# Input norm: the first third of the first product placed behind the third token tile, and the second token tile loaded ahead of the spread norm weights

## The chip, the cores and the metric

The kernel runs on one core of a Trainium2 chip. The metric is device time in microseconds (us). The core has a matrix engine (TensorE, PE in the profile; its weight loads are listed apart as PEld), a vector engine (VectorE, DVE), a scalar engine (ScalarE, ACT), a general engine (GpSimd, POOL) and a queue engine (SyncE, SP) that issues most DMAs. Each engine takes its own instructions in the written order and meets the others at semaphores.

## The reference

One step of a one-layer encoder. 1024 prompt tokens and 8 x 16 sample tokens, 1152 in all with 2048 features, are normed and multiplied by one wide input projection. From its columns come the inputs of a windowed attention and of a gated linear attention; both results are gated, joined, multiplied by an output projection and added to the input. Only the first two lines below are touched by this case.

```python
def rmsnorm(x, g):
    xf = x.astype(jnp.float32)
    y = xf * lax.rsqrt(jnp.mean(xf * xf, axis=-1, keepdims=True) + EPS)
    return (y * g.astype(jnp.float32)).astype(x.dtype)

    xn = rmsnorm(x, norm_g)          # (1024 + 128) x 2048
    h = xn @ w_in                    # 2048 x 5648
    ...
    return x + mix @ w_out           # 2048 x 2048
```

## The kernel before, in words

The 1152 tokens are nine tiles of 128 (`NT` = 9, numbered 0 to 8 here). The projection is computed transposed: an *item* j is a block of 128 output columns, and it is accumulated in three *groups* n of 384 tokens (`TN`), that is of three tiles each, over 16 slices k of the 2048 features. The product is taken in three passes per slice (lines 1835 to 1837: high part by low part, low by high, high by high), since both operands are held as a high part and a remainder (`x_hi`, `x_lo`, `w_hi`, `w_lo`). So item 0 has 3 x 16 x 3 matmuls.

Before any item can run, the *input norm* has to norm and turn the tiles. The work on tile t goes through four engines:

- **SP** loads the tile (`load_x`, line 344) into one of three buffers; from tile 3 on it first waits until the tile three before has been turned.
- **ACT** sums its squares (line 1666, "sum of squares t").
- **DVE** turns the sum into the variance (line 1969, "variance t"), **POOL** makes the reciprocal root (line 1621), and **DVE** scales the tile by it and by the norm weights `g_row` (line 1976, "scaling t"). The norm weights are one row of memory, spread by the DMA over 128 partitions, so that this transfer is as large as a tile (1024 KB).
- **PE** transposes the tile in 16 steps (line 1812, "turn t"), four to each of four PSUM banks.
- **ACT** copies each bank rounded to `x_hi` (line 1656), and **DVE** subtracts that from the bank to get `x_lo` (line 1963, `low_halves`). Only then may the bank be written by the next turn: `turn_x` waits for the `x_lo` of the tile before, bank by bank.

What fixes the order: each engine's list is written out by hand. ACT does the four copies of tile t and then sum of squares t + 2. DVE does scaling t, the first two `x_lo` of tile t - 1, variance t + 1, and the last two `x_lo` of tile t - 1. PE does turn t, and from tile 3 on puts a *third* of a group behind each turn: slices 0 to 5, 6 to 10 and 11 to 15 (18, 15 and 15 matmuls; here third A, B, C). Group 0 of item 0, which needs only the tiles 0, 1 and 2, stands behind the turns 3, 4 and 5; group 1 behind the turns 6, 7 and 8; group 2 follows as a whole. POOL splits the first item's weights into high part and remainder in between (lines 548 and 552), one of four chunks behind each reciprocal root from tile 1 to tile 4. All of this takes the first 58 us; after it, PE goes through items and then through the output projection.

Of the kernel before, what the change touches and what calls it, by code (L numbers as in the profile page):

```python
# [24 lines left out]
NT = TOK // P  # L25
# [3 lines left out]
NG = TOK // TN  # L29
# [53 lines left out]
def project(nc, sem, dram):  # L83
# [6 lines left out]
    with ExitStack() as ctx:  # L90
# [61 lines left out]
        s_xlo = sem("s_xlo")  # L152
# [186 lines left out]
        def _(sp):  # L339

            def load_x(t):
                if t >= 3:
                    sp.wait_ge(s_xt, 4 * (t - 2) + 4)
                sp.dma_start(x_buf[t % 3], x_p[t * P:t * P + P, :] if t < NTP else x_s).then_inc(s_x[t % 3], 16)

            load_x(0)
            sp.dma_start(g_row, norm_g[0:1, :].to_broadcast([P, D_MODEL])).then_inc(s_norm, 16)
            load_x(1)
            sp.dma_start(consts_sb[:, :], consts[:, 0:C_MASK0]).then_inc(s_ident, 16)
            load_x(2)  # L350
            for q in range(4):
# [145 lines left out]
            for q in range(4):  # L497
                load_w(q + 2, (q + 1) * P + (Q0 + P), P)
                store_item(q + 1, (q + 1) * P + Q0, P)
                ks = slice(4 * q, 4 * q + 4)  # L500
# [744 lines left out]
        class decode_pe:  # L1245
# [5 lines left out]
            def levels(self):  # L1251
                logits, values, diagonal, keys, level, _, _ = linear_stages(self.pe, T, dec=True)
                stages = {2: logits, 13: linear_stages(self.pe, T - 1)[-1], 17: diagonal, 21: keys, 38: values}
                for i, step in enumerate((28, 33)):
                    stages[step] = lambda i=i: level(i)
                return stages
# [188 lines left out]
        b_kp = work[:, 7136:7392].rearrange("p (c n) -> p c n", c=2)  # L1445
        b_mx, b_mn, b_neg, b_sk, b_es, b_sum, b_den = (small[:, 8 + 2 * i:10 + 2 * i] for i in range(7))
        kb, _, sb_, pb, nb = ub
        ob = sb_

# [353 lines left out]
        def _(pe):  # L1803
            pe.wait_ge(s_ident, 16)

            def turn_x(t):
                pe.wait_ge(s_xn, t + 1)
                for b in range(4):
                    pe.wait_ge(s_xlo, 4 * t + (b + 1))
                    for k in range(4):  # L1810
                        c = (4 * b + k) * P
                        mm = pe.transpose(xt_bank[b][:, k * P:k * P + P], x_buf[t % 3][:, c:c + P], ident)
                    mm.then_inc(s_xt, 1)
# [7 lines left out]
            def group(j, n, norm=False, norm_before=False, stages={}, ks=range(KT), sum_at=6):  # L1821

                pe.wait_ge(s_staged, NG * j + (n + 1))
                for k in ks:
                    if n * KT + k in stages:
                        stages[n * KT + k]()
                    if n == 0 and k % 4 == 0:
                        pe.wait_ge(s_wready, 4 * j + (k // 4 + 1))
                    if n > 0 and k == 6 and norm:
                        sum_squares(j, n - 1)  # L1830
                    if n == 0 and k == sum_at and norm_before:
                        sum_squares(j - 1, NG - 1)
                    tok = slice(n * TN, n * TN + TN)
                    out = acc[n][:, 0:TN]
                    pe.matmul(out, w_lo[:, k, :], x_hi[:, k, tok], start=(k == 0), stop=False)  # L1835
                    pe.matmul(out, w_hi[:, k, :], x_lo[:, k, tok], start=False, stop=False)  # L1836
                    mm = pe.matmul(out, w_hi[:, k, :], x_hi[:, k, tok], start=False, stop=(k == KT - 1))  # L1837
                    if n == NG - 1 and k % 4 == 3:
                        mm.then_inc(s_wfree, 1)
                if n < NG - 1 and ks[-1] == KT - 1:  # L1840
                    mm.then_inc(s_acc, 1)

            def sum_squares(j, n):
                pe.wait_ge(s_sqlo, j * NG + (n + 1))
                pe.wait_ge(s_v, j * NG + (n + 1))
                pe.matmul(ss_bank[:, 0:TN], ones_r, sq_lo, start=True, stop=False)
                pe.matmul(ss_bank[:, 0:TN], ones_r, sq_hi, start=False, stop=True).then_inc(s_ssq, 1)
# [25 lines left out]


            THIRDS = [range(0, 6), range(6, 11), range(11, KT)]
            for t in range(NT):
                turn_x(t)
                if t >= NG:
                    pe.wait_ge(s_xlo, 4 * t + 4)
                    group(0, t // NG - 1, ks=THIRDS[t % NG])  # L1880
            pe.wait_ge(s_xlo, 4 * NT + 4)
            pe.wait_ge(s_ones, 1)
            group(0, NG - 1, stages={(NG - 1) * KT + 2: lambda: sum_squares(0, 0),
# [72 lines left out]
        def _(dve):  # L1956
            dve.sem_inc(s_v, 1)
            dve.sem_inc(s_xlo, 4)
            def low_halves(t, banks=range(4)):
                for b in banks:  # L1960
                    dve.wait_ge(s_xhi, 4 * t + (b + 1))
                    dst = x_lo[:, 4 * b:4 * b + 4, t * P:t * P + P]
                    dve.tensor_tensor(dst, xt_bank[b][:, :].rearrange("p (k n) -> p k n", k=4),
                                      x_hi[:, 4 * b:4 * b + 4, t * P:t * P + P].bitcast(F32),
                                      ALU.subtract).then_inc(s_xlo, 1)

            def variance(t):
                dve.wait_ge(s_ss, t + 1)
                dve.tensor_scalar(var[:, :], ss[:, t % 2:t % 2 + 1], 1.0 / D_MODEL, EPS, ALU.mult, ALU.add)\
                   .then_inc(s_var, 1)  # L1970

            variance(0)
            dve.wait_ge(s_norm, 16)
            for t in range(NT):
                dve.wait_ge(s_rstd, t + 1)
                dve.scalar_tensor_tensor(out=x_buf[t % 3], in0=x_buf[t % 3], scalar=rstd[:, 0:1],
                                         in1=g_row, op0=ALU.mult, op1=ALU.mult).then_inc(s_xn, 1)
                if t >= 1:
                    low_halves(t - 1, range(2))
                if t + 1 < NT:  # L1980
                    variance(t + 1)
                if t >= 1:
                    low_halves(t - 1, range(2, 4))
            low_halves(NT - 1)
            dve.wait_ge(s_ident, 16)
# [259 lines left out]
```

## Time and profile before

| | |
|---|---|
| median of 3 runs | 1792.86 us (1791.85 to 1793.93) |
| the profiled execution's own time | 1792.29 us |
| its span, first to last instruction | 1790.5 us |
| PE busy | 1765.8 us (99%) |
| DVE, POOL, ACT busy | 781.5, 529.1, 505.2 us |
| mean granted TensorE clock | 0.996 |

PE is busy nearly all the time; the page's slices show a single one that stands out, the first (45 us), with PE at 6 tenths and its granted clock at 8 tenths. Engine times are busy times, and work on different engines overlaps. In a timeline, each row gives a start and a length, merged rows the length of the whole stretch, and the bracket tells how long the engine had been idle and which instruction let it go on. A row of PE ends later than the next one starts, since matmuls are pipelined.

### The profile page before, as it was taken

What the parts mean: (1) busy time and instruction counts of PE and PEld (TensorE: products, weight loads), DVE (VectorE), ACT (ScalarE), POOL (GpSimd) and SP (SyncE); (2) the same over time, 40 slices, a digit from 0 to 9 for tenths busy, and PEclk for the clock granted to TensorE, in tenths of its full rate; (3) what the DMA queues carried; (4) which work ended last, traced back from release to release, by engine and by line L of the source; (5) the groups of instructions that cost most, each with busy time, mean ns of one, the idle gap of its engine ahead of it and who ended that gap; (6) DMA issues with size and microseconds to landing.
All of it is one profiled execution on the core that took longest, in us unless ns stands there. A gap on an engine that the chain in (4) does not pass through costs nothing.

```text
span 1790.5 us, 29954 instructions
## 1 busy us (share of the span) xinstructions
PE 1765.8 (99%) x10741; PEld 1639.3 (92%) x10741; DVE 781.5 (44%) x1641; ACT 505.2 (28%) x1155; POOL 529.1 (30%) x486
## 2 busy tenths in 40 slices
PE   6999999999999999999999999999999999999999
PEld 5999999989999999999999999999999888888887
DVE  7754540554545421111556566552322453453433
ACT  6311110134333310000344434330011443343332
POOL 4356420322232242332655555552433000000000
PEclk8999999999999999999999999999999999999999
DMA  7432211343444332212333432334534675664654
GB/s 257 141 92 66 86 48 52 91 113 95 111 109 126 93 96 71 77 55 75 98 99 90 121 101 85 99 120 150 155 118 139 200 243 164 211 222 165 199 165 136
DMA packets 246128, 220.81 MB, mean 123 GB/s; under 512 B 26018, under 2 KB 210676, under 8 KB 244596
## 3 DMA queue, kind: packets, MB, share of 16 engines
q1 hardware_dynamic: 171828, 176.68, 31.4%
q10 hardware_dynamic: 74232, 43.23, 8.8%
q8 instruction: 42, 0.69, 0.2%
q14 instruction: 26, 0.21, 0.0%
HBM read 169.71 MB, written 52.24 MB: 124 GB/s over the span
## 4 chain that ended last, share of the span: by engine, by line
PE 96%; DVE 1%; DMA 1%; ACT 1%; ACTq 0%; issue 0%; POOL 0%; SPq 0%; DVEq 0%; POOLq 0%
PE p L1835 20%; PE p L1837 19%; PE p L1836 19%; PE p L1926 7%; PE p L1928 7%; PE p L1930 7%; PE p L901 2%; PE p L592 1%; PE p L1870 1%; PE p L1869 1%; PE p L1871 1%; PE p L620 1%; PE p L604 1%; PE p L913 1%; PE p L919 1%; PE p L912 1%
## 5 line engine op out<-in xcount | busy, mean ns | idle before, releaser
L1835 PE MATMUL p<-x_hi,w_lo 128*128 128x384 f32 x2016 | 697.6, 346 | 0.0
L1837 PE MATMUL p<-x_hi,w_hi 128*128 128x384 f32 x2016 | 675.3, 335 | 0.0
L1836 PE MATMUL p<-x_lo,w_hi 128*128 128x384 f32 x2016 | 674.3, 334 | 0.0
L1835 PEld LDWEIGHTS p<-x_hi,w_lo 128*128 128x128 f32 x2016 | 378.8, 188 | 15.6 <-issue 13.5
L548 POOL TENSOR_TENSOR w_hi<-raw,small 128x512 fp32r<-128x512 f32 x164 | 173.5, 1058 | 726.8 <-PE p L1837 710.8
L1836 PEld LDWEIGHTS p<-x_lo,w_hi 128*128 128x128 f32 x2016 | 379.1, 188 | 0.2
L1837 PEld LDWEIGHTS p<-x_hi,w_hi 128*128 128x128 f32 x2016 | 378.3, 188 | 0.0
L2137 DVE TENSOR_TENSOR w_lo<-raw,w_hi 128x512 fp32r<-128x512 f32 x192 | 132.1, 691 | 206.9 <-ACT w_hi L1783 206.9
L552 POOL TENSOR_TENSOR w_lo<-raw,w_hi 128x512 fp32r<-128x512 f32 x164 | 216.2, 1318 | 12.8
L1783 ACT ACTIVATE w_hi<-raw 128x512 fp32r<-128x512 f32 x192 | 120.8, 631 | 242.6 <-PE p L1930 213.1
L1926 PE MATMUL p<-w_hi,x_lo 128*128 128x512 f32 x570 | 160.2, 389 | 0.0
L1928 PE MATMUL p<-w_lo,x_hi 128*128 128x512 f32 x570 | 160.1, 389 | 0.0
L1930 PE MATMUL p<-w_hi,x_hi 128*128 128x512 f32 x570 | 160.1, 389 | 0.0
L1926 PEld LDWEIGHTS p<-w_hi,x_lo 128*128 128x128 f32 x570 | 106.9, 188 | 22.5 <-DVE w_lo L2137 0.4
L1928 PEld LDWEIGHTS p<-w_lo,x_hi 128*128 128x128 f32 x570 | 107.0, 188 | 22.3
L1930 PEld LDWEIGHTS p<-w_hi,x_hi 128*128 128x128 f32 x570 | 107.0, 188 | 22.2
L2023 DVE RECIPROCAL xn<-xn 128x384 f32<-128x384 f32 x30 | 76.6, 2553 | 18.9 <-ACT xn L1684 18.9
L2040 DVE TENSOR_TENSOR xn<-xn 128x384 f32<-128x384 f32 (+1 forms) x48 | 41.5, 879 | 99.1 <-ACT xn L1689 99.1
L2006 DVE COPY xn<-p 128x384 f32<-128x384 f32 x36 | 20.1, 557 | 132.6 <-PE p L1837 117.5
L1689 ACT ACTIVATE xn<-p 128x384 f32<-128x384 f32 x48 | 22.6, 491 | 175.5 <-PE p L1837 175.4
L745 DVE CUSTOM_DVE_ANT_0 work<-p,work,sink_row 128x192 f32<-128x192 f32 x128 | 45.7, 413 | 30.1 <-PE p L592 28.0
L679 ACT ACTIVATE work<-p 128x384 f32<-128x384 f32 x64 | 31.5, 492 | 91.5 <-PE p L605 91.3
(191 smaller groups left out, 1784.1 us busy)
## 6 DMA issues: line engine op xcount, KB each, us to landing
raw<-in_w_out SPq DMA_DIRECT2D x192, 256.0 KB, 3.5
raw<-in_w_in SPq DMA_DIRECT2D x164, 256.0 KB, 4.3
h_t<-xn SPq DMA_DIRECT2D x126, 192.0 KB, 1.9
work<-h_t SPq DMA_DIRECT2D x24, 384.0 KB, 6.1
out<-work SPq DMA_DIRECT2D x36, 256.0 KB, 4.6
work<-h_t ACTq DMA_DIRECT2D x16, 512.0 KB, 4.6
work<-h_t ACTq DMA_DIRECT2D x32, 256.0 KB, 4.2
work<-in_x_prompt SPq DMA_DIRECT2D x32, 256.0 KB, 4.9
```

What stands on the lines that cost most here:

```text
L548: pool.tensor_tensor(w_hi[:, k:k + 4, 0:n], w_raw(j, k, n), zeros[:, :].unsqueeze(1) .to_broadcast([P, 4, n]), ALU.add).then_inc(s_whi, 1)
L552: pool.tensor_tensor(w_lo[:, k:k + 4, 0:n], w_raw(j, k, n), w_hi[:, k:k + 4, 0:n].bitcast(F32), ALU.subtract).then_inc(s_wready, 1)
L745: dve.tensor_tensor_reduce(out=a_p[i][:, r, :], in0=bank_s[r % 2][:, (r // 2) * SPAN:(r // 2) * SPAN + SPAN], in1=a_mask[:, 2 * (r % 2), : ...
L1783: act.activation(o_hi[k % 4], o_raw[k % 4], ACT.Copy).then_inc(t_whi, 1)
L1835: pe.matmul(out, w_lo[:, k, :], x_hi[:, k, tok], start=(k == 0), stop=False)
L1836: pe.matmul(out, w_hi[:, k, :], x_lo[:, k, tok], start=False, stop=False)
L1837: mm = pe.matmul(out, w_hi[:, k, :], x_hi[:, k, tok], start=False, stop=(k == KT - 1))
L1926: pe.matmul(out[t], x_lo[:, k, tok[t]], o_hi[k % 4], start=(k == 0), stop=False)
L1928: pe.matmul(out[t], x_hi[:, k, tok[t]], o_lo[k % 4], start=False, stop=False)
L1930: mm = pe.matmul(out[t], x_hi[:, k, tok[t]], o_hi[k % 4], start=False, stop=(k == KT - 1))
L2023: dve.reciprocal(stage[n], tmp_b).then_inc(s_nchain, 1)
L2137: dve.tensor_tensor(o_lo[k % 4], o_raw[k % 4], o_hi[k % 4].bitcast(F32), ALU.subtract)\
```

## The change

Three lists are rewritten; no instruction is added or removed.

```diff
             load_x(0)
+            load_x(1)
             sp.dma_start(g_row, norm_g[0:1, :].to_broadcast([P, D_MODEL])).then_inc(s_norm, 16)
-            load_x(1)
...
             THIRDS = [range(0, 6), range(6, 11), range(11, KT)]
-            for t in range(NT):
+            for t in range(NG):
                 turn_x(t)
-                if t >= NG:
-                    pe.wait_ge(s_xlo, 4 * t + 4)
-                    group(0, t // NG - 1, ks=THIRDS[t % NG])
+            pe.wait_ge(s_xlo, 4 * NG + 4)
+            group(0, 0, ks=THIRDS[0])
+            turn_x(3)
+            group(0, 0, ks=THIRDS[1])
+            turn_x(4)
+            turn_x(5)
+            group(0, 0, ks=THIRDS[2])
+            for t in range(2 * NG, NT):
+                turn_x(t)
+                pe.wait_ge(s_xlo, 4 * t + 4)
+                group(0, 1, ks=THIRDS[t % NG])
...
             for t in range(NT):
+                if t == NG:
+                    low_halves(t - 1)
                 dve.wait_ge(s_rstd, t + 1)
                 dve.scalar_tensor_tensor(out=x_buf[t % 3], in0=x_buf[t % 3], scalar=rstd[:, 0:1],
                                          in1=g_row, op0=ALU.mult, op1=ALU.mult).then_inc(s_xn, 1)
-                if t >= 1:
+                if t >= 1 and t != NG:
                     low_halves(t - 1, range(2))
                 if t + 1 < NT:
                     variance(t + 1)
-                if t >= 1:
+                if t >= 1 and t != NG:
                     low_halves(t - 1, range(2, 4))
```

On the SP queue, at the start of the program, the second tile (buffer `raw`) and the spread norm weights change places:

```order
 L344 DMA work<-in_x_prompt 128x2048
-L347 DMA work<-in_norm_g 128x2048
 L344 DMA raw<-in_x_prompt 128x2048
+L348 DMA work<-in_norm_g 128x2048
 L349 DMA consts_sb<-in_consts 128x260
```

The second transfer is now the tile, the third the norm weights; both are of the same size.

On PE, from the end of turn 2 (buffer `xn`) on, where p_3 to p_6 are the banks of a turn and p_0 is the accumulator of group 0. Before:

```order
L1812 MATMUL p_5<-consts_sb,xn 128x128 x4
L1812 MATMUL p_6<-consts_sb,xn 128x128 x4
L1812 MATMUL p_3<-consts_sb,work 128x128 x4
L1812 MATMUL p_4<-consts_sb,work 128x128 x4
L1812 MATMUL p_5<-consts_sb,work 128x128 x4
L1812 MATMUL p_6<-consts_sb,work 128x128 x4
L1835 MATMUL p_0<-x_hi,w_lo 128x384
L1836 MATMUL p_0<-x_lo,w_hi 128x384
```

And the same place now:

```order
L1812 MATMUL p_5<-consts_sb,xn 128x128 x4
L1812 MATMUL p_6<-consts_sb,xn 128x128 x4
L1835 MATMUL p_0<-x_hi,w_lo 128x384
L1836 MATMUL p_0<-x_lo,w_hi 128x384
L1837 MATMUL p_0<-x_hi,w_hi 128x384
L1835 MATMUL p_0<-x_hi,w_lo 128x384
L1836 MATMUL p_0<-x_lo,w_hi 128x384
L1837 MATMUL p_0<-x_hi,w_hi 128x384
```

Third A, 18 matmuls, moved from behind turn 3 to ahead of it; third B moved from behind turn 4 to ahead of it in the same way.

On PE, two tiles later, at the turns 4 (buffer `raw`) and 5 (buffer `xn`). Before:

```order
L1836 MATMUL p_0<-x_lo,w_hi 128x384
L1837 MATMUL p_0<-x_hi,w_hi 128x384
L1812 MATMUL p_3<-consts_sb,xn 128x128 x4
L1812 MATMUL p_4<-consts_sb,xn 128x128 x4
L1812 MATMUL p_5<-consts_sb,xn 128x128 x4
L1812 MATMUL p_6<-consts_sb,xn 128x128 x4
L1835 MATMUL p_0<-x_hi,w_lo 128x384
```

And now:

```order
L1812 MATMUL p_3<-consts_sb,raw 128x128 x4
L1812 MATMUL p_4<-consts_sb,raw 128x128 x4
L1812 MATMUL p_5<-consts_sb,raw 128x128 x4
L1812 MATMUL p_6<-consts_sb,raw 128x128 x4
L1812 MATMUL p_3<-consts_sb,xn 128x128 x4
L1812 MATMUL p_4<-consts_sb,xn 128x128 x4
L1812 MATMUL p_5<-consts_sb,xn 128x128 x4
L1812 MATMUL p_6<-consts_sb,xn 128x128 x4
L1835 MATMUL p_0<-x_hi,w_lo 128x384
```

Before, third B stood between the turns 4 and 5; now the two turns stand next to each other. From turn 6 on the list is what it was.

On DVE, around scaling 3 (buffer `work`). Before:

```order
L1969 TENSOR_SCALAR small<-small 128x1
L1963 TENSOR_TENSOR x_lo<-p_5,x_hi 128x4x128
L1963 TENSOR_TENSOR x_lo<-p_6,x_hi 128x4x128
L1976 SCALAR_TENSOR_TENSOR work<-work,small 128x2048
L1963 TENSOR_TENSOR x_lo<-p_3,x_hi 128x4x128
L1963 TENSOR_TENSOR x_lo<-p_4,x_hi 128x4x128
L1969 TENSOR_SCALAR small<-small 128x1
L1963 TENSOR_TENSOR x_lo<-p_5,x_hi 128x4x128
L1963 TENSOR_TENSOR x_lo<-p_6,x_hi 128x4x128
L1976 SCALAR_TENSOR_TENSOR raw<-raw,small,work 128x2048
```

And now, where the lines have moved down by 8 and 10:

```order
L1977 TENSOR_SCALAR small<-small 128x1
L1971 TENSOR_TENSOR x_lo<-p_5,x_hi 128x4x128
L1971 TENSOR_TENSOR x_lo<-p_6,x_hi 128x4x128
L1971 TENSOR_TENSOR x_lo<-p_3,x_hi 128x4x128
L1971 TENSOR_TENSOR x_lo<-p_4,x_hi 128x4x128
L1971 TENSOR_TENSOR x_lo<-p_5,x_hi 128x4x128
L1971 TENSOR_TENSOR x_lo<-p_6,x_hi 128x4x128
L1986 SCALAR_TENSOR_TENSOR work<-work,small 128x2048
L1977 TENSOR_SCALAR small<-small 128x1
L1986 SCALAR_TENSOR_TENSOR raw<-raw,small,work 128x2048
```

All four `x_lo` of tile 2 stand ahead of scaling 3 now, and scaling 4 follows scaling 3 with only a variance between them.

## Rows read from the trace of the kernel before

**Rows 1.** The page of the kernel before: busy time and share by engine.

```profile
PE 1765.8 (99%) x10741; PEld 1639.3 (92%) x10741; DVE 781.5 (44%) x1641; ACT 505.2 (28%) x1155; POOL 529.1 (30%) x486
```

**Rows 2.** Waits of PE, 0 to 150 us: engine, line, releaser: total, times, longest.

```profile
PE p L1812 <- DVE work L1976: 11.2, 1, 11.2
PE p L1812 <- DVE x_lo L1963: 6.2, 4, 2.6
```

**Rows 3.** Timeline of PE: start, length, engine, line, operation, [idle before <- releaser].

```profile
11.21 3.44 PE L1812 MATMUL p<-consts_sb,work 128*128 128x128 f32 x16 [11.21 <-DVE work L1976]
...
22.58 3.65 PE L1812 MATMUL p<-consts_sb,xn 128*128 128x128 f32 x16 [2.60 <-DVE x_lo L1963]
...
27.63 3.91 PE L1812 MATMUL p<-consts_sb,work 128*128 128x128 f32 x16 [1.40 <-DVE x_lo L1963]
...
31.21 0.49 PE L1835 MATMUL p<-x_hi,w_lo 128*128 128x384 f32 x1
...
34.50 1.91 PE L1812 MATMUL p<-consts_sb,raw 128*128 128x128 f32 x16
...
38.86 2.32 PE L1812 MATMUL p<-consts_sb,xn 128*128 128x128 f32 x16
...
40.93 0.42 PE L1835 MATMUL p<-x_hi,w_lo 128*128 128x384 f32 x1
...
43.63 2.26 PE L1812 MATMUL p<-consts_sb,work 128*128 128x128 f32 x16
```

**Rows 4.** Timeline of PE, 55 to 60 us: first matmul of item 0's group 2.

```profile
57.70 0.33 PE L1835 MATMUL p<-x_hi,w_lo 128*128 128x384 f32 x1
```

**Rows 5.** Windows: length, busy (x) of five engines, granted clock, DMA.

```profile
16.00:18.00 2.00, 1.16 (x8) 0.83 (x8) 1.92 (x5) 1.84 (x4) 1.92 (x2) 0.93 0.77 137
18.00:20.00 2.00, 1.97 (x8) 1.57 (x8) 1.84 (x2) 1.07 (x2) 1.92 (x4) 0.50 1.00 418
...
30.00:32.00 2.00, 2.00 (x12) 2.00 (x11) 2.00 (x2) 1.23 (x3) 1.92 (x2) 0.66 0.14 57
```

**Rows 6.** Timeline of DVE, 0 to 80 us.

```profile
8.76 2.35 DVE L1976 SCALAR_TENSOR_TENSOR work<-work,small 128x2048 f32<-128x2048 f32 x1 [0.84 <-POOL small L1621]
...
18.72 3.12 DVE L1976 SCALAR_TENSOR_TENSOR xn<-xn,small,work 128x2048 f32<-128x2048 f32 x1 [0.16 <-POOL small L1621]
...
24.21 2.67 DVE L1976 SCALAR_TENSOR_TENSOR work<-work,small 128x2048 f32<-128x2048 f32 x1
...
28.79 0.15 DVE L1969 TENSOR_SCALAR small<-small 128x1 f32<-128x1 f32 x1 [0.70 <-ACT work L1666]
...
35.36 2.34 DVE L1976 SCALAR_TENSOR_TENSOR xn<-xn,small,work 128x2048 f32<-128x2048 f32 x1
...
39.19 1.28 DVE L1963 TENSOR_TENSOR x_lo<-p,x_hi 128x512 fp32r<-128x512 f32 x2
...
45.10 2.34 DVE L1976 SCALAR_TENSOR_TENSOR raw<-raw,small,work 128x2048 f32<-128x2048 f32 x1
...
52.07 4.91 DVE L1963 TENSOR_TENSOR x_lo<-p,x_hi 128x512 fp32r<-128x512 f32 x8
```

**Rows 7.** Timeline of ACT, 0 to 80 us.

```profile
10.71 1.91 ACT L1666 ACTIVATE work<-raw 128x2048 f32<-128x2048 f32 x1 [2.98 <-DMA raw<-in_x_prompt]
...
15.18 1.90 ACT L1666 ACTIVATE work<-xn 128x2048 f32<-128x2048 f32 x1
...
37.06 1.94 ACT L1666 ACTIVATE work<-work 128x2048 f32<-128x2048 f32 x1
```

**Rows 8.** Timeline of POOL, 0 to 80 us.

```profile
16.90 1.27 POOL L552 TENSOR_TENSOR w_lo<-work,w_hi 128x512 fp32r<-128x512 f32 x1
...
19.77 3.21 POOL L552 TENSOR_TENSOR w_lo<-work,w_hi 128x512 fp32r<-128x512 f32 x1
```

**Rows 9.** SP, when it issues a transfer: start, length, line.

```profile
1.21 0.42 SPq L347 DMA_DIRECT2D work<-in_norm_g  x1
```

**Rows 10.** DMA issues, 0 to 30 us: KB each, median us to landing.

```profile
work<-in_norm_g SPq DMA_DIRECT2D x1, 1024.0 KB, 7.0
```

## The prediction

> **What bounds the kernel now.** I read the page first: PE is busy 99% of the span [rows 1], so time can only be won or lost where PE stands idle or slow. The waits of PE over the first 150 us name only two causes: 11.2 us until scaling 0 on DVE is done, and 6.2 us in four waits for `x_lo`, also DVE [rows 2]. Both lie inside the input norm. The timeline of PE places them: idle to 11.21, 2.60 ahead of turn 2, 1.40 ahead of turn 3, then an unbroken stream, third A from 31.21, turn 4 at 34.50, turn 5 at 38.86, third C from 40.93, turn 6 at 43.63 [rows 3], and group 2 of item 0 at 57.70 [rows 4]. From that point PE does not wait in these rows, so the whole question is at what time group 2 of item 0 starts after the change. A shift of that start moves the end one for one.
>
> The second thing to see is the clock. It was granted at 0.50 (1.2 GHz) in 18 to 20 us, after two us in which PE had been busy for 1.16, and it rose inside 30 to 32 us (mean 0.66) [rows 5], at the end of turn 3, after 3.6 us without a pause. A turn of 16 transposes took 3.44 and 3.65 us early on and 1.91 us afterwards [rows 3]: 0.215 against 0.119 us each. I call 0.86 and 0.48 us the slow and fast time of a bank.
>
> The third thing is the loop that feeds PE. For each tile DVE needs a scaling (2.34 us alone, 2.67 and 3.12 elsewhere), four `x_lo` (eight in 4.91 us, 0.61 each) and a variance (0.15) [rows 6]. From scaling 5 at 35.36 to scaling 7 at 45.10 is 9.74 us, 4.87 a tile [rows 6]; PE spends 1.91 us of turn and about 2.8 us of third. The two are nearly level, so DVE has no slack to give back a delay.
>
> **The first edit, the norm weights behind tile 1.** SP issues the spread weights at 1.21 and they land 7.0 us later, at 8.2 [rows 9, 10]; tile 1, next in line and as large, lands at 10.71, where ACT ends its wait for it [rows 7]. Scaling 0 started at 8.76, with POOL's root as its last releaser [rows 6]. With the places swapped I let the landings swap: tile 1 at 8.2, weights at 10.7. Scaling 0 then runs from 10.7 to 13.1 instead of 8.76 to 11.1, and turn 0, which began at 11.21, from 13.15 to 16.6. The earlier tile 1 buys nothing: its sum of squares was not what PE waited for.
>
> Most of those 2 us survive. Sum of squares 2 stands on ACT behind the copies of turn 0: 15.18 becomes 17.3 (last bank 16.6, plus copy) and it ends at 19.3 [rows 7]. Variance 2 waits for it (as a variance did for ACT at 28.79, 0.70 us [rows 6]), and DVE's second pair of `x_lo` of tile 0 is queued behind that variance: 19.4 to 20.7. Scaling 2 goes from 18.72 to 20.7 [rows 6], turn 2 from 22.58 to 24.4, ending at 27.9 at the slow clock. Cost so far 1.8 us. Below, it could cost nothing if the three transfers landed together by 8.8; above, the whole 2.45 us between the two landings.
>
> **The second edit, third A ahead of turn 3.** It takes the place of the 1.40 us wait, and this is its gain. But it needs all `x_lo` of tile 2, so DVE does these four first: the last copy of turn 2 ends at 28.6 (27.9 plus 0.1 plus 0.6), the last `x_lo` at 29.2. Third A starts at 29.2 and scaling 3 too, 5.0 us later than its 24.21 [rows 6], ending by 31.8 under cover of third A. Third A's 18 matmuls took 3.29 us at the fast clock (31.21 to 34.50 [rows 3]). If the clock rises near 31.3 again, 2.1 us of it run slow; no row shows such a matmul slow, so I scale by the transposes, 0.18 times 1.8 gives 0.33 each: six are done by 31.3, the other twelve take 2.1. Third A ends at 33.3 and turn 3 at 35.2. Before, the same two pieces were done at 34.50: 0.7 us late. The bounds of this term are 0.4 us (all fast: 29.2 + 3.3 = 32.5, then turn 3 to 34.4, a gain of 0.1 against before) and all slow, 29.2 + 5.9, 1.8 us more than I take.
>
> **The third edit, turns 4 and 5 side by side.** This is the largest term. Third B goes ahead of turn 4, 35.2 to 37.9 (2.7 us, as 36.2 to 38.9 before). Scaling 4 is no obstacle: 32.7 to 35.3. Behind the copies of turn 3 (to 35.9) ACT does sum of squares 5 to 37.9; variance 5 and the second pair of `x_lo` of tile 3 follow at 38.1 to 39.3, so turn 4 ends at 39.8 and scaling 5 runs from 39.3 to 41.65 instead of from 35.36 [rows 6]. Before, turn 4 and third B were done at 38.86: 0.9 us late.
>
> Turn 5 now needs three things in a row that nothing covers: scaling 5, then the first `x_lo` of tile 4 (42.25), then, behind sum of squares 6 (40.4 to 42.4) and variance 6, the second pair, to 44.2, and a last bank of 0.48. It ends at 44.7. Before, the same loop ran from the end of turn 4 (34.50 + 1.91 = 36.4) to third C at 40.93, 4.5 us, with 2.7 us of third B inside it; sum of squares 6 at 37.06 and the pair at 39.19 are its links [rows 6, 7]. Now it is 4.9 us from 39.8 with nothing inside: PE is idle 2.4 us and then waits between banks. Third C (40.93 to 43.63, 2.7 us) ends at 47.4 instead of 43.63: 3.7 us late.
>
> **The rest.** The list from turn 6 on is unchanged, and DVE sets the pace. Scaling 6 stands behind the pair that ends at 44.2; scaling 7 comes 4.7 later at 48.9; from scaling 7 to the last block of `x_lo` it was 45.10 to 52.07, 6.97 us, so 55.9; the four of tile 7 take 2.45, the last bank of turn 8 another 0.5, third C 2.7. Group 2 starts at 61.5 instead of 57.70. The weight load of item 1 waits for turn 7, and its split for group 2 itself, so they move along.
>
> Sum: 61.5 - 57.7 = **3.8 us**. Against the profiled execution that is 1792.29 + 3.8 = 1796.1. The median of before is 0.57 above that execution, and the measured median is what the new one will be held against, so I predict 1792.86 + 3.8 = **1796.7 us**, 0.21% slower. About 0.2%, 3.6 us, is what can be told from no change here, so the forecast sits on that edge.
>
> **A rule weighed.** Scaling 2 took 3.12 us and POOL's subtraction beside it 3.21, while the same forms took 2.35 and 1.27 at other places [rows 6, 8]. The Trainium skill, GPSIMD Engine Reference, section Specifications, says that POOL shares its memory interfaces with VectorE and contends with instructions that read two SBUF operands, as a scaling does and an `x_lo`, with one operand in PSUM, does not. The trace agrees (3.12 against 2.35). By that rule scaling 2 stays slow at its new place, since POOL's next split starts behind root 2 at about 20, and the sum stays 3.8; without it the chain to turn 2 would be 0.8 shorter and the sum near 3.0.
>
> **Rivals.**
>
> *The clock falls again.* It fell once after the gap ahead of turn 1 [rows 5]. Around turn 5 PE would now be idle for 2.4 us and half idle for another 2.4. Third C at the slow clock costs 2.2 us more (2.7 times 0.8), parts of turns 5 and 6 another 0.5 to 1.5. Group 2 then starts 2 to 4 us later still: 1799 to 1800. Against it: between the turns of 38.86 and 43.63 small waits did no harm. Chance 0.20.
>
> *The clock rises early.* Turn 2 from 24.4 to 27.9 has no pause and third A follows within 1.3 us; if it rises there, third A and turn 3 are 1 us shorter, and part of it reaches turn 4 and 5. Or the weights land sooner than 10.7. Sum 1.5 to 2.9, 1794.4 to 1795.8. Chance 0.25.
>
> *The chain is hidden anyway.* If PE had enough work stored up that the DVE chain has slack, nothing changes: 1792 to 1794. The level pace (4.87 against 4.7) speaks against it. Chance 0.08.
>
> *Faster.* PE-bound mechanism: the third fills the wait of 1.40 ahead of turn 3, and by keeping PE busy from turn 2 on raises the clock before turn 3, which then takes 1.91 instead of 3.65: 1.4 + 1.7 = 3.1 us, 1789.7. It decides from the point where the weights land by 8.8 and the loop between turns 4 and 5 closes within 2.4 us instead of 4.5. Neither is in the rows. Chance 0.06.
>
> *The forecast*, 3.0 to 5.0 us, 0.41.
>
> **How the numbers follow.** Slower by over 0.2% (above 1796.4): 0.20 from the falling clock, and 0.31 of the forecast's 0.41, in all 0.51. Faster: 0.05. The rest, 0.44, within 0.2%. The range takes in the forecast, most of the falling clock and most of the early rise: 1793.8 to 1799.8.
>
> **What the new profile would show.** Right: scaling 0 near 10.7 with the weights as its releaser; turn 0 near 13.1; scaling 3 near 29 and third A at the same time; a PE gap of over 2 us ahead of turn 5, waiting for scaling 5 or `x_lo`; group 2 near 61.5. Wrong: scaling 0 at 8.8 (the landings do not swap), turn 5 close behind turn 4, or a granted clock below 1.00 between 40 and 48 us (the first rival).

## The result

The changed kernel took 1795.57 us (median of 20 runs, 1794.39 to 1798.29) against 1793.33 us for the kernel before (20 runs, 1791.46 to 1794.43). The ratio is 1.0015, 95% interval 1.0009 to 1.0021: 2.7 us slower by the ratio (1.6 to 3.8), 2.24 us by the medians. 1796.7 us and +3.8 us had been forecast. The direction is clear of noise, the size about two thirds of the forecast. It lies below the forecast's own 3.0 to 5.0 us and inside the 1.5 to 2.9 us of the rival in which the clock rises early. Of the 20 runs, the twelve with a mean granted clock of 0.997 took 1794.39 to 1796.17 us, and the eight with 0.995 or 0.996 took 1796.28 to 1798.29; the execution profiled below is one of the twelve.

The profiled execution took 1795.21 us with a span of 1793.4 us. Its timeline of PE, where the rows of before stand in [rows 3]:

```profile
13.17 3.65 PE L1812 MATMUL p<-consts_sb,work 128*128 128x128 f32 x16 [13.17 <-DVE work L1986]
...
24.06 3.65 PE L1812 MATMUL p<-consts_sb,xn 128*128 128x128 f32 x16 [2.31 <-DVE x_lo L1971]
...
29.12 0.44 PE L1835 MATMUL p<-x_hi,w_lo 128*128 128x384 f32 x1 [1.41 <-DVE x_lo L1971]
...
32.35 1.91 PE L1812 MATMUL p<-consts_sb,work 128*128 128x128 f32 x16
...
36.71 2.33 PE L1812 MATMUL p<-consts_sb,raw 128*128 128x128 f32 x16
41.32 3.53 PE L1812 MATMUL p<-consts_sb,xn 128*128 128x128 f32 x16 [2.29 <-DVE x_lo L1971]
```

Turn 0 starts at 13.17 (before 11.21), turn 2 at 24.06 (22.58), third A at 29.12 ahead of turn 3, turn 3 at 32.35 (27.63), turn 4 at 36.71 (34.50), turn 5 at 41.32 after an idle time of 2.29 us (38.86, with none). The first matmul of group 2, 57.70 in [rows 4], is now at 61.28:

```profile
61.28 0.33 PE L1835 MATMUL p<-x_hi,w_lo 128*128 128x384 f32 x1
```

The timeline of DVE, answering to [rows 6]:

```profile
10.72 2.35 DVE L1986 SCALAR_TENSOR_TENSOR work<-work,small 128x2048 f32<-128x2048 f32 x1 [2.94 <-DMA work<-in_norm_g]
...
19.38 0.15 DVE L1977 TENSOR_SCALAR small<-small 128x1 f32<-128x1 f32 x1 [2.02 <-ACT work L1666]
...
20.64 2.67 DVE L1986 SCALAR_TENSOR_TENSOR xn<-xn,small,work 128x2048 f32<-128x2048 f32 x1
...
28.98 2.34 DVE L1986 SCALAR_TENSOR_TENSOR work<-work,small 128x2048 f32<-128x2048 f32 x1
...
32.05 3.12 DVE L1986 SCALAR_TENSOR_TENSOR raw<-raw,small,work 128x2048 f32<-128x2048 f32 x1 [0.66 <-POOL small L1621]
...
36.97 0.15 DVE L1977 TENSOR_SCALAR small<-small 128x1 f32<-128x1 f32 x1 [0.60 <-ACT work L1666]
...
38.24 2.34 DVE L1986 SCALAR_TENSOR_TENSOR xn<-xn,small,work 128x2048 f32<-128x2048 f32 x1
...
47.41 0.15 DVE L1977 TENSOR_SCALAR small<-small 128x1 f32<-128x1 f32 x1 [0.92 <-ACT work L1666]
```

Scaling 0 has a new releaser, the norm weights, and starts at 10.72 instead of 8.76. Two waits are new to DVE, or in a new place: 0.66 us for POOL's root 4 ahead of scaling 4 (32.05), and 0.60 us for ACT's sum of squares 5 (36.97). Scaling 5 starts at 38.24 instead of 35.36. ACT no longer waits 2.98 us for tile 1 [rows 7], which has landed by 8.22:

```profile
8.22 1.91 ACT L1666 ACTIVATE work<-raw 128x2048 f32<-128x2048 f32 x1 [0.62 <-DMA raw<-in_x_prompt]
```

The clock took another course than before. It fell near 21.0 us, was back near 27.8, and fell a second time inside 40 to 42, right behind the gap ahead of turn 5; for before see [rows 5], a fall near 18 and a rise near 31.

```profile
20.00:22.00 2.00, 1.56 (x8) 0.98 (x8) 2.00 (x3) 1.13 (x3) 1.92 (x3) 0.75 0.49 205
...
26.00:28.00 2.00, 1.71 (x8) 1.30 (x7) 1.68 (x3) 1.45 (x3) 1.48 (x2) 0.55 0.00 0
...
40.00:42.00 2.00, 0.68 (x4) 0.71 (x5) 2.00 (x5) 1.55 (x2) 0.09 (x1) 0.87 0.95 299
42.00:44.00 2.00, 2.00 (x11) 2.00 (x10) 2.00 (x3) 1.19 (x2) 0.46 (x1) 0.50 0.54 225
```

So 3.58 us of delay stand at group 2, but the spans differ by 2.9 us only. Part of it is given back much later. In the timeline of the weight loads of PE, one attention unit (line 620) stands at 411.97 and the next at 427.12 in before, and between them PE waited 0.45 us for ACT:

```profile
411.97 0.85 PEld L620 LDWEIGHTS p<-work 128*64 128x64 f32 x16 [0.25 <-issue]
...
424.54 0.20 PEld L604 LDWEIGHTS p<-consts_sb,work 128*128 128x128 f32 x2 [0.45 <-ACT work L679]
...
427.12 0.85 PEld L620 LDWEIGHTS p<-work 128*64 128x64 f32 x16 [0.25 <-issue]
```

In the changed kernel the same two stand at 415.55 and 430.37, with no such wait between them; the shift goes from 3.58 to 3.25 us:

```profile
415.55 0.85 PEld L620 LDWEIGHTS p<-work 128*64 128x64 f32 x16 [0.25 <-issue]
...
430.37 0.85 PEld L620 LDWEIGHTS p<-work 128*64 128x64 f32 x16 [0.25 <-issue]
```

### The profile page after: what moved, and what is told of

Its sections match the earlier page's. It is cut to its first block, busy times and chain, and to the rows that moved or that the text cites. A ratio compares the mean times of both kernels' runs of the same rounds, so it can differ in the third digit from the quotient of the medians.

```text
span 1793.4 us, 29952 instructions
## 1 busy us (share of the span) xinstructions
PE 1765.2 (98%) x10741; PEld 1639.5 (91%) x10741; DVE 781.2 (44%) x1641; ACT 504.5 (28%) x1155; POOL 526.8 (29%) x486
## 4 chain that ended last, share of the span: by engine, by line
PE 96%; DVE 1%; ACT 1%; DMA 1%; issue 0%; ACTq 0%; POOL 0%; SPq 0%; DVEq 0%; POOLq 0%
PE p L1835 20%; PE p L1837 19%; PE p L1836 19%; PE p L1934 7%; PE p L1936 7%; PE p L1938 7%; PE p L901 2%; PE p L592 1%; PE p L1870 1%; PE p L1869 1%; PE p L1871 1%; PE p L1812 1%; PE p L620 1%; PE p L604 1%; PE p L919 1%; PE p L913 1%
## 5 line engine op out<-in xcount | busy, mean ns | idle before, releaser
L2050 DVE TENSOR_TENSOR xn<-xn 128x384 f32<-128x384 f32 (+1 forms) x48 | 41.5, 879 | 99.3 <-ACT xn L1689 99.3
L679 ACT ACTIVATE work<-p 128x384 f32<-128x384 f32 x64 | 31.4, 491 | 91.1 <-PE p L605 91.0
```

## The experiments

For each kernel I read two numbers: its median, beside a kernel before run on the same chip, and the start of the first sum-of-squares matmul of group 2 of item 0 (line 1846), here "the mark". It is at 58.74 in before and 62.32 in the changed kernel, and nothing of the input norm comes after it on PE:

```profile
58.74 0.33 PE L1846 MATMUL p<-sq_parts 128*128 128x384 f32 x1
```

```profile
62.32 0.33 PE L1846 MATMUL p<-sq_parts 128*128 128x384 f32 x1
```

**1. The load order alone.**

```diff
             load_x(0)
+            load_x(1)
             sp.dma_start(g_row, norm_g[0:1, :].to_broadcast([P, D_MODEL])).then_inc(s_norm, 16)
-            load_x(1)
```

> Only the first edit: tile 1 is loaded ahead of the spread norm weights, the lists of PE and DVE are those of before. My step (the swap delays scaling 0 by 2 us and 1.8 us of that reach turn 2, and the DVE loop behind it has no slack): scaling 0 starts near 10.7, turn 2 near 24.2, group 2 of item 0 at 58.9 to 59.5 instead of 57.7, time 1.2 to 1.8 us above before. Rival (the early delay is taken up by the waits of 2.60 and 1.40 us ahead of turns 2 and 3): turn 3 stays near 27.6 and the time is within 0.5 us of before.

Measured: 1794.96 us against 1792.90, ratio 1.0012 (1.0003 to 1.0021). Turn 2 at 23.79, and turn 3 did not stay near 27.6:

```profile
23.79 3.65 PE L1812 MATMUL p<-consts_sb,xn 128*128 128x128 f32 x16 [1.91 <-DVE x_lo L1963]
29.13 3.64 PE L1812 MATMUL p<-consts_sb,work 128*128 128x128 f32 x16 [1.69 <-DVE x_lo L1963]
```

The mark is at 60.24, 1.50 us late. The step of the prediction holds (1.8 us expected at turn 2, 1.2 seen there; 1.2 to 1.8 us expected in time, about 2.1 measured, 0.5 to 3.8 by the interval of the ratio). The rival falls.

**2. The edits of PE and DVE alone** (the changed kernel with the loads of before).

```diff
             load_x(0)
-            load_x(1)
             sp.dma_start(g_row, norm_g[0:1, :].to_broadcast([P, D_MODEL])).then_inc(s_norm, 16)
+            load_x(1)
```

> Only the edits of PE and DVE: third A behind turn 2, third B behind turn 3, turns 4 and 5 side by side, all x_lo of tile 2 ahead of scaling 3; the norm weights are loaded ahead of tile 1 as before. My step (these cost about 2 us by themselves): third A starts near 27.4, scaling 3 near 27.3, a gap of over 2 us ahead of turn 5, time 1.0 to 2.5 us above before. Rival (the swap is the whole loss, and filling the wait of 1.40 us ahead of turn 3 is a gain): within 0.3 us of before or faster by up to 1.4 us.

Measured: 1795.12 us against 1792.90, ratio 1.0009 (1.0000 to 1.0019).

```profile
27.70 0.69 PE L1835 MATMUL p<-x_hi,w_lo 128*128 128x384 f32 x1 [1.41 <-DVE x_lo L1971]
...
32.60 1.91 PE L1812 MATMUL p<-consts_sb,work 128*128 128x128 f32 x16
```

Third A started at 27.70, but at the slow clock, so that turn 3 could start only at 32.60, later than in the full change (32.35), whose third A started 1.4 us later on a fast clock. The mark is at 62.63. The medians differ by 2.2 us (1.0 to 2.5 expected), and by the interval of the ratio by 0 to 3.4. The edits cost something by themselves, as forecast; but two parts that cost about 2 us each and about 2.2 together do not add up. The course of the clock lies over both.

**3. Third B back between turns 4 and 5**, on the kernel of experiment 2.

```diff
             turn_x(3)
-            group(0, 0, ks=THIRDS[1])
             turn_x(4)
+            group(0, 0, ks=THIRDS[1])
             turn_x(5)
```

> As the kernel with only the edits of PE and DVE, but with third B back between turns 4 and 5. Theory of the prediction (the side by side turns uncover the loop of turn 4, its copies, sum of squares 6, x_lo, turn 5, and that is the largest term): the gap of over 2 us ahead of turn 5 goes, third B runs inside it, and the time is 1.5 to 2.7 us below that kernel, so no slower than before. Rival (scaling 3, pushed behind the four x_lo of tile 2, moves the whole chain of DVE back by 3 us and the chain is what bounds; where third B stands only moves the idle time): the gap appears ahead of turn 4 instead, and the time is within 0.7 us of that kernel.

Measured: 1794.28 us against 1792.90, ratio 1.0007 (0.9998 to 1.0016), 0.8 us below experiment 2 and within the noise of the ratios: between what the two theories said (1.5 to 2.7 us, and within 0.7). The mark is at 61.08, 1.55 us earlier, at the edge of the first. The gap ahead of turn 5 went, but gaps ahead of turn 4 and inside it came in its place, as the rival had it:

```profile
34.56 1.17 PE L1812 MATMUL p<-consts_sb,raw 128*128 128x128 f32 x8 [1.66 <-DVE x_lo L1971]
36.41 1.97 PE L1812 MATMUL p<-consts_sb,raw 128*128 128x128 f32 x8 [0.69 <-DVE x_lo L1971]
```

PE was fast during third A here (18 matmuls from 27.76 to 30.99) and slow at its start in experiment 2 (27.70 to 32.60), so this pair does not decide.

**4. PE kept busy in the gap ahead of turn 5**, on the changed kernel.

```diff
+            def keep_busy(n):
+                for _ in range(n):
+                    pe.transpose(ss_bank[:, 0:P], ident, ident)
...
             turn_x(4)
+            keep_busy(16)
             turn_x(5)
```

> The changed kernel with 16 further transposes of the identity matrix, into a bank that nobody reads at that time, between turns 4 and 5; they fill the gap of 2.3 us in which the changed kernel's PE stood idle before its granted clock fell to 0.50 at 41.7 us. Clock theory: the clock stays at 1.00 through turn 5 and third C, turn 5 takes about 2.3 us instead of 3.53, and the time falls by 0.8 to 1.4 us against the changed kernel, to 1.0 to 1.6 us above before. Rival (the chain of DVE paces the turns whatever the clock): the clock stays up and the time is within 0.4 us of the changed kernel, 2.0 to 2.8 us above before.

Measured: 1795.51 us against 1792.90, ratio 1.0019 (1.0010 to 1.0028). In the profiled execution the clock stayed up:

```profile
40.00:42.00 2.00, 1.46 (x14) 1.13 (x12) 2.00 (x5) 1.67 (x2) 0.00 (x0) 1.00 0.92 283
42.00:44.00 2.00, 2.00 (x15) 1.58 (x15) 2.00 (x3) 1.84 (x4) 0.55 (x1) 1.00 0.58 242
```

The mark came at 61.42, 0.90 us earlier than 62.32, of the size expected. In time nothing is seen, 1795.51 against 1795.57 for the changed kernel in another session, and 2.6 us above before, where the rival had 2.0 to 2.8: the stretch from the mark to the end of the span is 1.2 us longer in this execution than in the changed kernel's (1732.3 against 1731.1). Four of its eleven runs lie at 1797 to 1798.5, with a mean granted clock of 0.996 or 0.997, and seven at 1795.1 to 1795.8, with 0.998; where the four lost the clock was not profiled. The experiment shows the clock's price at this one place, not a gain.

**5 to 8. The clock taken out of the comparison.** The same device, with more transposes, ahead of every long gap of PE, on four orders of work, run one after the other on one chip. First the kernel before:

```diff
                 turn_x(t)
+                if t < NG:
+                    keep_busy((8, 12, 10)[t])
```

> The kernel before with 8, 12 and 10 further transposes of the identity matrix behind turns 0, 1 and 2, into a bank nobody reads then, so that PE has no long gap from turn 0 on. Clock theory: the granted clock, once up, stays at 1.00; turns 2 and 3 and third A run at the fast rate, and the first sum-of-squares matmul of group 2, at 58.74 in before, comes 0.5 to 1.6 us earlier; the time is 0.5 to 1.6 us below before. Rival (the added transposes delay the turns as much as the clock gives): within 0.4 us of before.

Then the edits of PE and DVE without that of the loads:

```diff
             for t in range(NG):
                 turn_x(t)
+                keep_busy((8, 12, 6)[t])
...
             turn_x(4)
+            keep_busy(16)
             turn_x(5)
```

> The kernel with only the edits of PE and DVE (norm weights ahead of tile 1), with 8, 12, 6 and 16 further identity transposes behind turns 0, 1, 2 and 4, so that the clock is out of the comparison with the kernel before with such transposes. Theory A (side by side turns, 2.7 us uncovered): the sum-of-squares matmul comes 2 us or more behind that one's. Theory B (scaling 3 pushed back behind the x_lo of tile 2, partly caught up by DVE since PE's third A fills the wait): 0.8 to 1.5 us behind it. Theory C (all of the loss of the PE and DVE edits was the clock): within 0.3 us.

Then the same with third B back between turns 4 and 5:

```diff
             turn_x(3)
-            group(0, 0, ks=THIRDS[1])
+            keep_busy(12)
             turn_x(4)
-            keep_busy(16)
+            group(0, 0, ks=THIRDS[1])
             turn_x(5)
```

> As the previous kernel but with third B back between turns 4 and 5, and 8, 12, 6 and 12 further identity transposes behind turns 0, 1, 2 and 3. Theory A (side by side turns are the loss): its sum-of-squares matmul comes 1.5 to 2.7 us earlier than in the previous kernel. Theory B (the chain of DVE bounds, whatever stands between turns 4 and 5): within 0.4 us of it, and the idle time of PE lies ahead of turn 4 instead of turn 5.

And the whole change, the second of these with the loads swapped:

> The changed kernel in full, with 8, 12, 6 and 16 further identity transposes behind turns 0, 1, 2 and 4; against the kernel that differs from it only in loading the norm weights ahead of tile 1, this prices the first edit without the clock. My step (1.8 us at turn 2 that all survive): its sum-of-squares matmul comes 1.4 to 2.0 us later than there. Rival (the price of the swap is mostly hidden): within 0.5 us.

| kernel, with added transposes | median us (11 runs each) | mark | clock of the profiled run |
|---|---|---|---|
| 5. before | 1790.78 (1790.35 to 1791.58) | 57.40 | 1.000 |
| 6. edits of PE and DVE | 1791.98 (1791.64 to 1793.56) | 59.00 | 1.000 |
| 7. the same, third B back | 1792.54 (1791.55 to 1793.69) | 58.95 | 1.000 |
| 8. the whole change | 1793.51 (1793.34 to 1794.09) | 60.55 | 1.000 |

Plain before in the same session: 1793.22. The ratios to it are 0.9989 (0.9980 to 0.9998), 0.9998 (0.9989 to 1.0007), 0.9999 (0.9990 to 1.0008) and 1.0004 (0.9995 to 1.0013). The marks of kernels 5 to 8:

```profile
57.40 0.33 PE L1846 MATMUL p<-sq_parts 128*128 128x384 f32 x1
```

```profile
59.00 0.33 PE L1846 MATMUL p<-sq_parts 128*128 128x384 f32 x1
```

```profile
58.95 0.33 PE L1846 MATMUL p<-sq_parts 128*128 128x384 f32 x1
```

```profile
60.55 0.33 PE L1846 MATMUL p<-sq_parts 128*128 128x384 f32 x1
```

In kernel 5 the mark is 1.34 us earlier than in before (0.5 to 1.6 expected), and the median is 2.4 us lower, which is more than expected. Now the parts add up at the mark: 1.60 us for the PE and DVE edits, 1.55 for the loads, 3.15 in all; by the medians 1.20, 1.53 and 2.73. The runs of kernels 5 and 6 do not overlap. The place of third B gives 0.05 us, and its return made the median no better (+0.56). PE waits ahead of turn 4 and inside it instead (0.33 and 0.71 us). Theory A, the side by side turns, is out; theory B holds, though its size was put at 0.8 to 1.5 us and 1.60 came. The timeline of DVE says where the 1.6 us are. In kernel 5, scalings 3, 4 and 5:

```profile
24.23 2.67 DVE L1982 SCALAR_TENSOR_TENSOR work<-work,small 128x2048 f32<-128x2048 f32 x1
...
29.28 2.66 DVE L1982 SCALAR_TENSOR_TENSOR raw<-raw,small,work 128x2048 f32<-128x2048 f32 x1
...
34.33 2.33 DVE L1982 SCALAR_TENSOR_TENSOR xn<-xn,small,work 128x2048 f32<-128x2048 f32 x1
```

In kernel 6, the same three, with the variance that waited:

```profile
26.68 2.33 DVE L1992 SCALAR_TENSOR_TENSOR work<-work,small 128x2048 f32<-128x2048 f32 x1
...
29.74 3.12 DVE L1992 SCALAR_TENSOR_TENSOR raw<-raw,small,work 128x2048 f32<-128x2048 f32 x1 [0.67 <-POOL small L1621]
...
34.67 0.15 DVE L1983 TENSOR_SCALAR small<-small 128x1 f32<-128x1 f32 x1 [0.61 <-ACT work L1666]
...
35.93 2.34 DVE L1992 SCALAR_TENSOR_TENSOR xn<-xn,small,work 128x2048 f32<-128x2048 f32 x1
```

Scaling 3 is 2.45 us later (26.68 against 24.23), scaling 4 only 0.46, scaling 5 again 1.60. In kernels 5 to 8, and in 10 to 12 below, the mark comes 23.07 or 23.08 us after the start of scaling 5, whatever the order on PE: what delays scaling 5 delays the product. Behind scaling 3 nothing is left for DVE to do while POOL makes root 4 (0.67 us), and sum of squares 5 is waited for (0.61 us), because turn 3, on whose copies it stands, comes later; the one pair of `x_lo` before it is over too early. In kernel 5 neither wait is there. Scaling 4 is also longer, 3.12 us against 2.66. The reason stands in the rows of POOL: the same rounding of a weight chunk starts 0.52 us ahead of scaling 4 in kernel 5, and in kernel 6, where both wait for root 4, only 0.07 us ahead. So more of it overlaps the scaling (see the last section).

```profile
28.76 1.04 POOL L548 TENSOR_TENSOR w_hi<-work,small 128x512 fp32r<-128x512 f32 x1
```

```profile
29.67 1.04 POOL L548 TENSOR_TENSOR w_hi<-work,small 128x512 fp32r<-128x512 f32 x1
```

**9 and 11. DVE's edit alone.** PE's list of before with the added transposes, and on DVE all `x_lo` of tile 2 ahead of scaling 3:

```diff
             for t in range(NT):
+                if t == NG:
+                    low_halves(t - 1)
...
-                if t >= 1:
+                if t >= 1 and t != NG:
                     low_halves(t - 1, range(2))
...
-                if t >= 1:
+                if t >= 1 and t != NG:
                     low_halves(t - 1, range(2, 4))
```

> The list of PE as before with 8, 12 and 10 identity transposes behind turns 0, 1 and 2, and of the change only DVE's edit: all x_lo of tile 2 ahead of scaling 3. Theory D (the price of the PE and DVE edits lies on DVE: scaling 3 is 2.4 us later, and root 4 and sum of squares 5, formerly hidden behind x_lo of tile 2, are waited for with 0.7 and 0.6 us): the sum-of-squares matmul of group 2 comes 1.0 to 1.6 us after the 57.40 of the kernel that differs only in this edit. Rival (moving third A on PE is what costs, through turn 3): within 0.3 us of 57.40.

Measured: 1793.53 us against 1793.34, ratio 1.0000 (0.9991 to 1.0009), the mark at 60.05, 2.65 us behind kernel 5: more than expected. Turn 3 had waited 2.90 us for scaling 3, and it took 3.32 us; the clock had fallen in that wait. So the same with `keep_busy((8, 22, 30)[t])`:

> As the kernel with PE's list of before, identity transposes and only DVE's edit, but with 22 and 30 of them behind turns 1 and 2 instead of 12 and 10, since the clock had fallen at 29.2 us in the wait of 2.9 us ahead of turn 3. Theory D as first sized (the DVE edit alone costs 1.0 to 1.6 us once the clock is out of it): clock at 1.00 from turn 2 on, sum-of-squares matmul at 58.4 to 59.2 instead of 60.05. Rival (the 2.65 us seen there were all DVE): it stays at 59.7 or later.

Measured: 1791.72 us against 1793.43, ratio 0.9993 (0.9984 to 1.0002). Its turn 3, and on DVE its scaling 4 and the variance that waited in kernel 6:

```profile
29.15 1.97 PE L1812 MATMUL p<-consts_sb,work 128*128 128x128 f32 x16 [0.72 <-DVE work L1984]
```

```profile
29.82 3.12 DVE L1984 SCALAR_TENSOR_TENSOR raw<-raw,small,work 128x2048 f32<-128x2048 f32 x1 [0.66 <-POOL small L1621]
...
34.06 0.14 DVE L1975 TENSOR_SCALAR small<-small 128x1 f32<-128x1 f32 x1
```

```profile
58.40 0.33 PE L1846 MATMUL p<-sq_parts 128*128 128x384 f32 x1
```

Turn 3 takes 1.97 us, and the mark is at 58.40, 1.00 us behind kernel 5. So 1.0 of the 1.6 us is DVE's order, and the other 1.65 of the first try was the clock. The rival, that all of the 2.65 us were DVE's, falls. The rows also say what the 1.0 consists of: scaling 4 starts 0.54 us later than in kernel 5 (29.82 against 29.28), with the wait for root 4 in it, and takes 0.46 longer. The other 0.60 us of kernel 6 are its wait of 0.61 us for sum of squares 5. Kernel 11 has none there: its turn 3 starts at 29.15, and ACT ends that sum at 33.79, before DVE asks for it at 34.06; in kernel 6 turn 3 stands behind third A, starts at 30.04, and the sum ends at 34.63.

**10 and 12. Third A behind two banks only.** Slices 0 to 5 lie in banks 0 and 1. So third A waits for these two, and DVE keeps the other pair of `x_lo` behind variance 4, where it hides root 4 (kernel 6 changed; 12 has `(8, 22, 0)`):

```diff
-                keep_busy((8, 12, 6)[t])
-            pe.wait_ge(s_xlo, 4 * NG + 4)
+                keep_busy((8, 12, 0)[t])
+            pe.wait_ge(s_xlo, 4 * NG + 2)
...
                 if t == NG:
-                    low_halves(t - 1)
+                    low_halves(t - 1, range(2))
...
-                if t >= 1 and t != NG:
+                if t >= 1:
                     low_halves(t - 1, range(2, 4))
```

> PE's list of the change with 8, 12 and 16 identity transposes behind turns 0, 1 and 4, weights ahead of tile 1, but third A (slices 0 to 5, which lie in banks 0 and 1) waits only for the x_lo of these two banks of tile 2, and DVE does only these two ahead of scaling 3 and leaves the other two behind variance 4. Theory D (root 4 and sum of squares 5 are covered again): the chain of DVE stands as in the kernel before with added transposes, scaling 5 near 34.3, the sum-of-squares matmul at 56.9 to 57.6, time within 0.5 us of that kernel, though turns 4 and 5 are side by side and third A is ahead of turn 3. Theory A (side by side turns cost 2 us or more): at 59 or later.

Measured: 1791.44 us against 1793.34, ratio 0.9992 (0.9983 to 1.0001), the mark at 58.57, 1.17 us behind kernel 5 and a miss: 56.9 to 57.6 was expected. The clock was down from 23.8 to 27.2 us, so third A ran slow at first, and turn 3, sum of squares 5 and scaling 5 (35.49 against 34.33 in kernel 5) came late again:

```profile
34.23 0.15 DVE L1983 TENSOR_SCALAR small<-small 128x1 f32<-128x1 f32 x1 [0.93 <-ACT work L1666]
```

> As the kernel whose third A waits for two banks only, but with 22 identity transposes behind turn 1 instead of 12, since its clock had fallen from 23.9 to 27.1 us. If the fall is why it came 1.17 us behind the kernel before with added transposes: clock at 1.00 from turn 1 on, third A over by 28.5, sum-of-squares matmul at 57.0 to 57.8, time 1790.3 to 1791.0. Rival (the side by side order costs a wait for sum of squares 5 of its own): it stays at 58.2 or later.

Measured: 1791.01 us against 1793.43, ratio 0.9988 (0.9979 to 0.9997); third A at 25.72, turn 3 at 28.97, the mark just outside what was expected (57.0 to 57.8):

```profile
57.93 0.33 PE L1846 MATMUL p<-sq_parts 128*128 128x384 f32 x1
```

At 57.93 it is 0.53 us behind kernel 5, with turns 4 and 5 still side by side. Root 4 is hidden again; two thirds of the loss of kernel 6 (1.60 us) are gone. Of the 0.53 left, 0.33 stand at the start of scaling 4 (29.61 against 29.28) and 0.2 between it and variance 5, for which sum of squares 5 is a little late. Kernels 5 and 12 are the two that beat both the kernel before and the changed one: 0.11% (0.02 to 0.20%) and 0.12% (0.03 to 0.21%) faster than before. They ran in different sessions and can't be told apart; by the mark, kernel 5 is the better one, and it is the kernel before with 30 idle transposes and nothing else.

## Why the prediction was right, and where it was wrong

**The first edit: right.** Scaling 0 was forecast at 10.7 and came at 10.72, turn 0 at 13.15 and came at 13.17, turn 2 at 24.4 and came at 24.06. It cost 1.55 us at the mark and 1.53 in the median with the clock out of the way (kernels 6 and 8), near the 1.8 forecast at turn 2. That the earlier tile 1 buys nothing is borne out: variance 2 stands waiting 2.02 us for ACT's sum of squares 2, which comes behind the copies of the delayed turn 0, as the prediction had it. Turn 2 was 0.34 us early mainly because scaling 2 took 2.67 us and not the 3.12 that it was held to. The prediction saw the 3.12 beside POOL's subtraction. A subtraction was beside scaling 2 again (from 21.24), but only 0.52 us of the POOL instruction ahead of it were left when scaling 2 started, and that is what counts (last section).

**The second edit: the start right, the cost wrong.** Third A and scaling 3 were forecast at 29.2 and came at 29.12 and 28.98. The clock was put at a rise near 31.3 and rose near 27.8, so turn 3 started at 32.35 instead of 33.3. Turn 3 was over at 34.26, 0.24 us ahead of the 34.50 of before, where 0.7 us late had been forecast; the lower bound is called 0.4 us in the prediction, but the sum beside it gives a gain of 0.1. The second rival (the clock rises early) came true in this execution.

**The third edit: the gap right, its cause wrong.** A gap of 2.4 us ahead of turn 5 was forecast, and 2.29 came. But the sentence "This is the largest term", with "4.9 us from 39.8 with nothing inside", took a symptom for the cause. Third B back in that gap wins nothing (58.95 against 59.00): PE then waits ahead of turn 4. The cost sits a tile earlier, on DVE, in scaling 3 pushed behind four `x_lo`: with the clock level, 1.0 of 1.6 us come with DVE's edit alone (root 4 uncovered, and scaling 4 beside more of POOL's work), and 0.6 with third A ahead of turn 3, through sum of squares 5. The times worked out for DVE contained this (scaling 5 forecast 4 us late, 2.9 measured); the name of the term did not. The first rival (the clock falls again) came true as well: the clock fell near 41.5 and turn 5 took 3.53 us; at the mark that was worth 0.90 us (experiment 4), where the rival had 2 to 4. The two clock rivals, thought of as alternatives, happened in one execution and nearly cancelled: scaling 6 started at 42.95, 1.25 us ahead of the 44.2 forecast, then DVE waited 0.92 us for sum of squares 7 behind the slow turn 5 (47.41 above), and scaling 7 started at 48.67, close to the 48.9 forecast.

**The sum.** Group 2 was forecast at 61.5 and came at 61.28, +3.58 us. That it came so close is in part luck, by the two clock terms above: with the clock level the whole change moves the mark by 3.15 us; the slow clock adds 1.77 us at the mark in the changed kernel (62.32 against 60.55) and 1.34 in before (58.74 against 57.40). The step that mis-sized the result is "A shift of that start moves the end one for one": the profiled spans differ by 2.9 us only. Of the 0.7 us lost on the way, 0.33 are given back at one wait near 424 us. The medians differ by 2.24. The 0.7 us between 2.9 and 2.24 come from setting one execution against another: before's profiled execution was 1.0 us under its median of 20, and the changed kernel's 0.4 under its own. With the clock level, the whole change costs 2.73 us by the medians; that the ratio says 2.7 too may be chance, since its interval is 1.6 to 3.8.

**What stays open.** The stretch from the mark to the end of the span is not constant: over the fourteen kernels it lies between 1730.9 us (experiments 3 and 11) and 1732.4 (kernel 5), with 1731.8 in before and 1731.1 in the changed kernel. Most of this spread of 1.5 us is two waits of PE. One is that for ACT near 424 us, which kernel 5 has as before has it, and experiment 3 has not. The other lies in the output projection, for DVE's `w_lo`: 1.15 us in kernel 5, 0.38 in before, 0.29 in the changed kernel, none in experiment 3. In kernel 5:

```profile
1573.64 0.53 PEld L1932 LDWEIGHTS p<-w_hi,x_lo 128*128 128x128 f32 x3 [1.15 <-DVE w_lo L2143]
```

Why these waits come and go is open; they limit what can be told from the time of one execution, and the marks are free of them. Where the clock fell in the longer runs of experiment 4 and of the changed kernel is open too.

## What to carry to other kernels

Where two engines feed each other at nearly the same pace, filling the idle time of one with work that makes the other do its list in another order is no gain: ask which small step (a root on a third engine, a sum on a fourth) the old order was hiding, and what hides it now. A gap that opens behind an edit need not be where the loss is; put the work back into it and see whether the gap only moves. And where changes of 0.1% are compared near the start of a program, first level the clock in all variants with idle work, and see in the profile that it stayed up (in experiments 9 and 10 it had not), or parts that cost 1.5 and 1.2 us will each look like 2 and together like 2.

## What the runs showed of the hardware

- A matmul of 384 columns on the slow clock started every 0.32 us against 0.17 on the fast one; the prediction had scaled it to 0.33 from the transposes. In the kernel of experiment 10, from slow to fast within one third:

```profile
26.27 0.52 PE L1837 MATMUL p<-x_hi,w_hi 128*128 128x384 f32 x1
26.59 0.52 PE L1835 MATMUL p<-x_hi,w_lo 128*128 128x384 f32 x1
...
27.38 0.34 PE L1835 MATMUL p<-x_hi,w_lo 128*128 128x384 f32 x1
27.55 0.34 PE L1836 MATMUL p<-x_lo,w_hi 128*128 128x384 f32 x1
```

- The granted clock fell in gaps of PE and came back under work at different points for nearly the same schedule: it was slow from 17.7 to 31.4 us in before and from 21.0 to 27.8 in the changed kernel (by windows of 1 us).
- Ahead of its first fall the column of the clock does not tell the rate. It shows 1.00 from the start in every kernel, but turn 0 took 3.4 to 3.7 us in every kernel, which is the slow rate. In experiment 3, whose column falls only near 36.4, turns 1 and 2 were slow as well (3.65 and 3.60 us); third A, at 27.76, was the first fast work. The length of a turn has to be read beside the column:

```profile
22.74 3.60 PE L1812 MATMUL p<-consts_sb,xn 128*128 128x128 f32 x16 [2.27 <-DVE x_lo L1971]
```

- With thirty idle transposes in gaps of PE (kernel 5; 1.63, 1.47 and 1.25 us by their rows) the column stayed at 1.00, and turns 2 and 3 took 2.42 us each instead of 3.65 and 3.91. The median was 2.4 us lower (1790.78 against 1793.22), and most of the spread was gone (1.2 us against 4.0, of 11 and 33 runs). Of the 2.4 us the marks show 1.34.
- A scaling takes 2.33 us with POOL idle, and it is longer by nearly what is left of the POOL instruction that is running when it starts: 0.52 us left, 2.66 us (scaling 4 of kernel 5); 0.70 left, 2.83 (scaling 3 of kernel 12); 0.97 left, 3.12 (scaling 4 of kernel 6). A subtraction that POOL starts during a scaling does not lengthen it further, but takes 3.2 us itself instead of 1.27 and ends 1.2 us after the scaling; scalings 3 and 4 of kernel 5, both with a subtraction beside them, took 2.67 and 2.66. The Trainium skill, GPSIMD Engine Reference, section Specifications, names the cause (interfaces shared with VectorE, contention with instructions of two SBUF inputs), and these rows agree. In the changed kernel the slow one moved from scaling 2 to scaling 4, which the prediction had kept at scaling 2.
